# The last two picks of an expert gather, in five parts of 120, 8, 9, 105 and 14 rows

## The reference

```
u = expert_down[idx]                       # idx: 128 tokens x 8 heads x 16 experts, per block
act = gelu(einsum('td,thkd->thk', xb, u))
vv = expert_up[idx]
x = x + einsum('thk,thkd->td', gate * act, vv)
```

## Time and profile before

| | us |
|---|---|
| median of three runs | 1270.63 |
| lowest and highest | 1269.94, 1271.02 |
| the profiled execution, its own time | 1269.91 |
| its span in the profile | 1268.2 |

### The profile page before, as it was taken

One profiled execution on the slowest core, in us unless ns is written; L12 is line 12 of the kernel. 1 busy time (PEld: TensorE's weight loads), 2 busy tenths in 40 slices (PEclk: granted clock), 3 DMA queues, 4 the chain that ended last, 5 costly groups with the idle time before them and its releaser, 6 DMA issues.

```text
span 1268.2 us, 15414 instructions
## 1 busy us (share of the span) xinstructions
PE 1172.7 (92%) x5672; PEld 818.9 (65%) x5672; DVE 711.9 (56%) x1512; ACT 622.5 (49%) x1344; POOL 752.9 (59%) x481
## 2 busy tenths in 40 slices
PE   9999999999998677787799798889999999999998
PEld 8987999965553233333355353443599998888887
DVE  5443135399686675766859678665546533422223
ACT  8586555544434232234424553554654675544442
POOL 7696668645553344554444445454247678788885
PEclk9999999999999898889999999999999999999999
DMA  8553446999999999999999999999524446565542
GB/s 278 193 197 117 149 151 240 370 376 426 425 424 424 424 424 424 424 424 425 424 421 425 424 424 424 416 418 424 218 88 159 134 137 196 167 199 194 181 157 100
DMA packets 121996, 381.78 MB, mean 301 GB/s; under 512 B 8512, under 2 KB 66880, under 8 KB 89152
## 3 DMA queue, kind: packets, MB, share of 16 engines
q0 software_dynamic: 36864, 268.45, 50.7%
q1 hardware_dynamic: 83584, 112.25, 26.7%
q10 hardware_dynamic: 1472, 0.09, 0.1%
HBM read 379.72 MB, written 1.05 MB: 300 GB/s over the span
## 4 chain that ended last, share of the span: by engine, by line
PE 65%; DMA 20%; DVE 7%; ACT 4%; POOL 2%; issue 1%; ACTq 0%; DVEq 0%; POOLq 0%
DMA rows_w<-peer_rows_in,arena 17%; PE ps L1140 15%; PE ps L835 13%; PE ps L864 8%; PE ps L1391 6%; PE ps L1444 4%; PE ps L1395 3%; PE ps L1193 3%; DVE rows_w L2527 3%; PE ps L1344 2%; PE ps L1369 2%; POOL rows_w L778 1%; DMA arena<-peer_rows_in,arena 1%; PE ps L1214 1%; ACT wgt L1770 1%
## 5 line engine op out<-in xcount | busy, mean ns | idle before, releaser
L565 POOL TENSOR_TENSOR w_lo<-ring,w_hi 128x1024 fp32r<-128x1024 f32 x178 | 434.1, 2456 | 160.1 <-ACT w_hi L559 160.0
L1140 PE MATMUL ps<-rows_w,diag 128*128 128x512 f32 x672 | 324.5, 622 | 57.1 <-ACT diag L1779 57.1
L778 POOL DMA_INDIRECT rows_w<-peer_rows_in,arena x168 | 195.4, 1163 | 233.5 <-PE ps L1140 196.9
L1140 PEld LDWEIGHTS ps<-rows_w,diag 128*128 128x128 f32 x672 | 128.1, 199 | 220.4 <-issue 136.6
L2527 DVE CUSTOM_DVE_ANT_0 rows_w<-rows_w,arena 128x1024 f32<-128x1024 f32 x168 | 203.5, 1224 | 103.3 <-DMA rows_w<-peer_rows_in,arena 102.7
L559 ACT ACTIVATE w_hi<-ring 128x1024 fp32r<-128x1024 f32 x178 | 184.1, 1058 | 105.2 <-PE ps L1395 45.5
L1768 ACT ACTIVATE gelu<-dots,rr 128x4 f32<-128x4 f32 (+2 forms) x91 | 27.0, 296 | 318.6 <-DVE dots L2527 318.1
L1140 PE MATMUL ps<-arena,diag 128*128 128x512 f32 x260 | 124.3, 607 | 13.6 <-ACT diag L1779 13.5
L778 POOL DMA_INDIRECT arena<-peer_rows_in,arena x66 | 76.0, 1151 | 59.6 <-PE ps L1140 51.2
L2527 DVE CUSTOM_DVE_ANT_0 arena<-arena 128x1024 f32<-128x1024 f32 x66 | 80.5, 1224 | 37.8 <-DMA arena<-peer_rows_in,arena 37.6
L1140 PEld LDWEIGHTS ps<-arena,diag 128*128 128x128 f32 x260 | 48.5, 194 | 75.0 <-issue 54.1
(11 more groups left out here) (468 smaller groups left out, 2042.6 us busy)
## 6 DMA issues: line engine op xcount, KB each, us to landing
ring<-w_in_in SPq DMA_DIRECT2D x38, 1024.0 KB, 5.2
ring<-w_ffn_gate_in SPq DMA_DIRECT2D x11, 1024.0 KB, 5.3
ring<-w_ffn_up_in SPq DMA_DIRECT2D x11, 1024.0 KB, 5.3
ring<-w_ffn_down_in SPq DMA_DIRECT2D x11, 1024.0 KB, 4.9
ring<-w_out_in SPq DMA_DIRECT2D x8, 1024.0 KB, 7.2
ring<-w_branch_attn_in SPq DMA_DIRECT2D x4, 1024.0 KB, 5.3
ring<-w_branch_mlstm_in SPq DMA_DIRECT2D x4, 1024.0 KB, 5.2
arena<-w_in_in SPq DMA_DIRECT2D x2, 2048.0 KB, 12.1
```

The lines of the kernel that those rows point to most:

```text
L565: pool.tensor_tensor(lo_of(n, u)[:, t, 0:cols], raw_half(n, g)[:, t, 0:cols], hi_of(n, u)[:, t, 0:cols].bitcast(F32), ALU.subtract).then_i ...
L778: pool.indirect_dma_start(pick_row(p, 0, 2 * D), None, a["peer_rows"], bass.IndirectOffsetOnAxis(ap=idx[:, g // PH, j:j + 1], axis=0)).the ...
L1140: ins = pe.matmul(acc[:, c, :], diag[:, p % 4, :], pick_row(p, D + c * CW, CW), start=(p == first), stop=True, skip_group_check=True)
```

## The change

Pick 255 is no longer issued in its turn. At pick 254 GpSimd waits for the place of pick 255 as well, and for three small transfers, and then issues five indirect DMAs in place of two: rows 0 to 119 of pick 254, rows 120 to 127 of it, rows 105 to 113 of pick 255, rows 0 to 104 of it, rows 114 to 127 of it. The semaphores of the two places count 32 and 48 instead of 16 for these picks, and `landed` says so. The row numbers of the three parts that do not begin at row 0 are first moved to partition 0 and following, into the new tile `idx_moved`, by three transfers of 8, 9 and 14 numbers that SP issues when `routed` has reached 12, ahead of its waits for the ring.

```diff
+        LAST_PARTS = ((PICKS - 2, 0, 120),
+                      (PICKS - 2, 120, 128),
+                      (PICKS - 1, 105, 114),
+                      (PICKS - 1, 0, 105),
+                      (PICKS - 1, 114, 128))
+        moved = [part for part in LAST_PARTS if part[1]]
...
         def landed(p):
-            return 16 * PLACE[:p + 1].count(PLACE[p])
+            return 16 * (PLACE[:p + 1].count(PLACE[p]) + max(0, [part[0] for part in LAST_PARTS].count(p) - 1))
...
                 if n == NPEER:
+                    sp.wait_ge(sem("routed"), (NB * PH - 1) // PR + PR + 3)
+                    for k, (q, first, last) in enumerate(moved):
+                        sp.dma_start(idx_moved[0:last - first, k:k + 1], idx[first:last, NB - 1, q - PICKS // NB:q - PICKS // NB + 1]).then_inc(sem("idx_moved"), 16)
                     sp.wait_ge(sem("row_free"), 1 + max(last_pick(q) for q in RAW_SLOTS))
...
                     j = g % PH * TOPK + k
+                    if p == LAST_PARTS[-1][0]:
+                        continue
+                    if p == LAST_PARTS[0][0]:
+                        pool.wait_ge(sem("row_free"), taken_last(PICKS - 1) + 1)
+                        pool.wait_ge(sem("idx_moved"), len(moved) * 16)
+                        for q, first, last in LAST_PARTS:
+                            at = idx_moved[0:last - first, moved.index((q, first, last)):moved.index((q, first, last)) + 1] if first else \
+                                idx[0:last, NB - 1, q - PICKS // NB:q - PICKS // NB + 1]
+                            pool.indirect_dma_start(pick_row(q, 0, 2 * D)[first:last], None, a["peer_rows"],
+                                                    bass.IndirectOffsetOnAxis(ap=at, axis=0)).then_inc(row_sem(q), 16)
+                        continue
                     pool.indirect_dma_start(pick_row(p, 0, 2 * D), None, a["peer_rows"],
                                             bass.IndirectOffsetOnAxis(ap=idx[:, g // PH, j:j + 1], axis=0)).then_inc(row_sem(p), 16)
```

More of the change, by code:

```diff
@@ L369, in build @@
         lev_mask = sb("lev_mask", [P, len(LEVELS) - 1, P])
+        idx_moved = sb("idx_moved", [P, 4], U32)
         eps_col = sb("eps_col", [P, 1])
```

## The result

| | before | after |
|---|---|---|
| median | 1270.32 us (1269.94 to 1271.02, 4 runs) | 1278.82 us (1277.12 to 1279.72, 4 runs) |
| profiled execution, its span | 1269.91, 1268.2 | 1278.51, 1276.8 |

The ratio is 1.0065, with a 95% interval of 1.0049 to 1.0081: 8.5 us slower. I had forecast 1270.0 with a range up to 1272.1, and gave 0.08 to slower.

What follows compares the result with a forecast made beforehand. Full DMA engines in the gather, then the chain from pick 255's landing to the last sum, were taken as the bound. 1269.91 less 0.63 gave 1269.3; with the median 0.7 above, 1270.0; range 1268.9 to 1272.1.

Steps and rivals of the forecast that it cites:

- What bounds, and where.: Gather with full DMA engines; gains or losses before the last sum at 899.91 reach the end one for one, nothing else.
- Dot 253 still starts at 893.04 (its gather is not changed).: DVE's queue ahead of dot 254: dot 253 unmoved, then two subtractions, so dot 254 starts at 894.82, 0.63 us earlier.
- a later dot 253: Sign of being wrong: issue or small transfers cost what had been put at nothing; no size given.
- Spreading the rows: Gathers of picks 254 and 255: late engine relieved of 13 rows, pick 255 seen 2.5 us earlier; forecast chance 0.62.
- doubled row time: Rival at the split gathers: engines writing the same part of SBUF go at half speed; +1.2 us, chance 0.12.
- its case of 1.5 times the row time: Engines fall out of step in the split gathers: pick 255 seen at 897.3, nothing left of the gain.
- a share near 0.5: Sign for doubled row time: DMA share near 0.5 in 888 to 895.
- late engine not spared: Rival at the split gathers: the late engine has 17 rows, both landings 0.3 us later; +0.3, chance 0.14.
- The low clock.: A chance stretch of lower clock would make the kernel slower; 0.01 given to it, no size in us.
- Few engines: Rival: a count 16 doesn't divide goes to few engines; on one, the end comes 25 us later; chance 0.07.
- Waits, issue and small transfers at 0: GpSimd's later issue and the three transfers before the last picks cost 0; the transfers at most 0.3 us.
- the gain of 0.63 capped by DVE and TensorE: Before the last sum: DVE's subtractions and product 253 hold back pick 254, so 2.5 us of landing gain only 0.63.

Runs made afterwards that it cites:

- the gathers alone: Kernels with only gathers of expert-table rows, no blocks computed and zeros as output: 128 rows ran at 416 GB/s, 120 rows at 212.
- the whole picks: Changed kernel with picks 254 and 255 gathered whole, added waits and three small transfers kept: 1270.99 us, 1.0003 to the kernel before.
- the short rows: Kernel before, picks 254 and 255 whole and in turn, but only 1024 floats of each row read: 1269.83 us, 0.9997.
- the marked kernel: Changed kernel with pick 254 in parts of 112, 2, 2, 2, 2, 8 rows and 255 in 120, 2, 2, 2, 2: 1277.46 us, one run.

## Why the prediction was wrong

- *What bounds, and where.* Right: nothing changed outside the stretch before the last sum.
- *"Dot 253 still starts at 893.04 (its gather is not changed)."* This step failed. Its gather is not changed, but dot 253 came 6.25 us later: three quarters of the result. Splitting 254 or 255 alone showed that their parts do this, with 253 whole (2.2 and 4.2 us). How they do it is argued from the gathers alone: the late engines still carry rows of 253 while the early ones already write those of 254 and 255, and groups of partitions are shared between engines, whichever gather a row is of. Among my signs, a later dot 253 stood for the issue or the small transfers; the whole picks excluded that.
- *"Spreading the rows": the late engine relieved of 13 rows, chance 0.62.* Wrong twice. Rows took twice as long (213 GB/s at full share; 212 for 120 rows alone), and the spared engine was not the late one: it had 17 rows. I took "equal shares of whole rows" from gathers that are all of one shape, which can't show what the shape does.
- *The rival "doubled row time", 0.12, +1.2 us.* The right mechanism, far too cheap. I reckoned it only from the second latest engine and only for the split picks, and then halved it for engines out of step. The latest engine and the picks ahead were not in the sum, nor what TensorE's standing still does to its clock. A smaller slip is in its case of 1.5 times the row time: 897.3 is when the engine ends, and DVE would see it at 897.8. The sign named for it was wrong too: not a share near 0.5, but a full share at half the GB/s. "In the trace nothing speaks for it" was true, and a rule of the Trainium skill stood beside it; a missing row is no reason for a low price.
- *The rival "late engine not spared", 0.14.* It happened, and its price was right: at full clock the last sum is 7.19 behind dot 253 for 6.87 before, 0.32 later, where I had 0.3. Sparing that engine is worth 1.01 at full clock (7.19 to 6.18; my two terms, 0.63 and 0.3, give 0.93) and 0.06 at low clock (8.90 to 8.84).
- *The low clock.* I gave it 0.01 as chance. It followed from the wait: 3.20 us without a matmul ahead of product 252, and products 253 and 254 took 6.41 us for 3.70. Its price behind dot 253 is 1.7 to 1.9 us in the profiled executions; the medians don't show it.
- *"Few engines".* Excluded by the packet counts, which fit 120 and 105 rows on 15 engines each.
- *Waits, issue and small transfers at 0; the gain of 0.63 capped by DVE and TensorE.* Both right, by the whole picks and by the short rows.

The change could hardly have paid. Its best case was worth 0.6 to 0.7 us behind dot 253, and every split that was tried, all of side-by-side partitions, cost 5.4 us or more. Parts with partitions 4 apart, which ran at full rate by themselves, were not tried in the kernel. None of the variants beats the kernel before; the nearest (short rows) leaves work out and can't be told from it.

## What to carry to other kernels

Where transfers keep all engines full, the shape of a part is a price of its own: ask which partitions the engines write at the same time, not only how many rows each has. A transfer that is made slow also slows those ahead of it that are still in the queues, so look for its cost in picks that the change doesn't touch. And before a transfer is moved or split to land earlier, ask what is next in line: here 2.5 us of landing were reckoned at 0.63, and the short rows gave 0.68 in the trace and nothing that the time shows.

## What the runs showed of the hardware

- A gather to every fourth partition with 8 rows at a time reached 408 GB/s, nearly the 416 of 128 rows, while 8 rows side by side got 106 and 120 rows 212.
- One engine of the 16 ended the stage some 3 us behind all others in the kernel before and in that with whole picks. In the marked kernel the late one was the fourth in the turn, and with that one spared the last two dots no longer waited for a DMA. The Trainium skill's "DMA: Bandwidth & Descriptors", section "Latency and other measured facts", names engines 7 and 15 as the usually slower ones; if the turn starts at engine 0, the runs here disagree. Why it is late stays open.
- Within the slow stretch the rate fell to 147 to 197 GB/s for some microseconds, below the half that sharing between two would give, and dot 253 moved by up to two microseconds between runs of like kernels. Which engines meet when was not measured.
